# The sums of the down projection's weight quarters, made on GpSimd in place of VectorE

## What is computed

```
def conv_ffn(a, w_up, conv_w, w_down):
    g, u = jnp.split(dwconv3(a @ w_up, conv_w), 2, axis=-1)
    return (jax.nn.silu(g) * u) @ w_down
...
h = h + g2 * conv_ffn(modulate(rms_norm(h, norm_ffn[i]), sh2, sc2), ffn_w_up[i], ffn_conv[i], ffn_w_down[i])
```

## Time and profile before

| | before |
|---|---|
| median of three runs | 1985.34 us |
| the profiled execution | 1986.11 us, its span 1984.3 us |
| TensorE (PE) | 1875.4 us, 95% of the span |
| VectorE (DVE) | 909.3 us, 46% |
| ScalarE (ACT) | 371.8 us, 19% |
| GpSimd (POOL) | 25.1 us, 1% |
| DMA | 466.33 MB, 235 GB/s on the mean |
| granted clock of TensorE | 0.974 |

### The profile page before, as it was taken

The page is one execution under the profiler, slowest core; times in us unless marked ns, Lnnn a source line. Parts: engine busy times, 40 slices in busy tenths (PEclk is TensorE's granted clock), DMA queues, the critical chain, the costliest instruction groups (busy, mean ns, idle before and its releaser), DMA issues.

```text
span 1984.3 us, 45659 instructions
## 1 busy us (share of the span) xinstructions
PE 1875.4 (95%) x20976; PEld 1639.5 (83%) x20976; DVE 909.3 (46%) x1566; ACT 371.8 (19%) x691; POOL 25.1 (1%) x24
## 2 busy tenths in 40 slices
PE   6999987989998999997999998999999989999998
PEld 4788776889997688785989997667888988878898
DVE  3868786100004758765100004575667661134355
ACT  3012232100002022232100003163211101021110
POOL 0000200000000000200000000000000000000000
PEclk8999998999999999998999999999999999999999
DMA  9994547699995673543799994211878553435330
GB/s 359 387 386 157 192 167 282 234 361 404 423 413 202 220 261 129 204 178 133 300 388 410 423 405 149 85 43 43 283 270 296 199 206 119 136 127 170 122 113 23
DMA packets 180613, 466.33 MB, mean 235 GB/s; under 512 B 5152, under 2 KB 55680, under 8 KB 172288
## 3 DMA queue, kind: packets, MB, share of 16 engines
q1 hardware_dynamic: 180192, 463.83, 62.9%
q10 hardware_dynamic: 288, 0.52, 0.1%
HBM read 463.29 MB, written 1.05 MB: 234 GB/s over the span
## 4 chain that ended last, share of the span: by engine, by line
PE 87%; DVE 8%; ACT 2%; issue 1%; DMA 1%; SPq 0%; DVEq 0%; ACTq 0%
PE pair L395 86%; DVE AR L1557 1%; DMA ring<-in_ada_w 1%; PE pair L1034 1%; DVE RST L1612 1%; DVE AR L1795 1%; DVE XH L2186 1%; ACT AR L1279 1%; DVE XH L1557 1%; DVE AR L1805 0%; SPq L286 0%; PE pair L903 0%; DVE AR L1809 0%; DVE XH L1796 0%; DVE AR L1787 0%
## 5 line engine op out<-in xcount | busy, mean ns | idle before, releaser
L395 PE MATMUL pair<-XH,ring 128*128 128x256 f32 (+1 forms) x3328 | 751.4, 387 | 19.2 <-ACT XH L1180 17.3
L395 PEld LDWEIGHTS pair<-XH,ring 128*128 128x128 f32 (+1 forms) x3328 | 629.6, 191 | 126.0 <-issue 30.4
L395 PE MATMUL pair<-AR,ring 128*64 128x88 f32 (+2 forms) x14336 | 700.5, 249 | 19.0 <-issue 14.9
L395 PEld LDWEIGHTS pair<-AR,ring 128*64 128x64 f32 (+1 forms) x14336 | 670.8, 140 | 42.6 <-issue 22.9
L2044 DVE TENSOR_TENSOR AR<-AR,pair 128x352 f32<-128x352 f32 x32 | 16.7, 521 | 428.9 <-PE pair L395 428.9
L1557 DVE SCALAR_TENSOR_TENSOR AR<-ring,CACT,AR 128x512 f32<-128x512 f32 x245 | 184.2, 752 | 8.7
L395 PE MATMUL pair<-AR 128*64 128x128 f32 (+5 forms) x1472 | 145.4, 302 | 6.2 <-ACT AR L1446 3.3
L395 PEld LDWEIGHTS pair<-AR 128*64 128x64 f32 (+3 forms) x1472 | 116.2, 152 | 17.9 <-issue 4.2
L2242 DVE SCALAR_TENSOR_TENSOR AR<-pair,VEC,AR 128x255 f32<-128x255 f32 x88 | 41.9, 476 | 96.2 <-ACT AR L1471 96.2
L1379 ACT ACTIVATE AR<-pair 128x704 f32 (+1 forms) x32 | 24.4, 762 | 306.1 <-PE pair L395 306.1
L1471 ACT ACTIVATE AR<-pair,VEC 128x256 f32<-128x256 f32 x88 | 36.6, 467 | 217.9 <-PE pair L395 217.9
(11 more groups left out here) (268 smaller groups left out, 1199.9 us busy)
## 6 DMA issues: line engine op xcount, KB each, us to landing
ring<-in_ada_w SPq DMA_DIRECT2D x48, 2048.0 KB, 13.1
ring<-in_w_gate SPq DMA_DIRECT2D x32, 2048.0 KB, 10.4
ring<-in_w_up SPq DMA_DIRECT2D x32, 2048.0 KB, 10.6
ring<-in_w_down SPq DMA_DIRECT2D x32, 2048.0 KB, 11.3
ring<-in_ffn_w_up SPq DMA_DIRECT2D x44, 1024.0 KB, 7.6
ring<-in_w_in SPq DMA_DIRECT2D x18, 2048.0 KB, 14.4
ring<-in_ffn_w_down SPq DMA_DIRECT2D x8, 2048.0 KB, 8.0
ring<-in_sc_w_in SPq DMA_DIRECT2D x6, 2048.0 KB, 7.9
```

Source lines behind the costliest of these rows:

```text
L395: return pe.matmul(o, lhsT, rhs, start=start, stop=stop, **kw)
```

## The change

The function `weight_sums` and its calls are gone from VectorE's list. GpSimd's list gets, after its work in the first block, a wait for the last chunk of the attention's output weights, and then the same four sums for all twelve chunks, in one row and with the same buffers and semaphores.

```diff
-            def weight_sums(l, n, since=0, upto=4):
...
-                    if j == 20:
-                        weight_sums(l, 0)
...
                 token_sums(l, 2)
-                for n_ in (1, 2):
-                    weight_sums(l, n_)
-                weight_sums(l, 3, upto=3)
                 output(X, l, 0)
-                weight_sums(l, 3, since=3)
                 if l == 0:
                     for t in range(1, 4):
                         fold(H, t, t == 6)
-                for n_ in (4, 5):
-                    weight_sums(l, n_)
                 output(X, l, 1, H if l == 0 else None)
...
+            pool.wait_ge(s["multiplied"], ck("wwo", 1) + 1)
+            for l in range(DEPTH):
+                for n in range(6):
+
+                    i, c = 6 * l + n, ck(f"down{n}", l)
+                    n_p = DOWN_PAIRS[n % 3][1]
+                    a11, a12, a21, a22 = weight_blocks(c, n_p)
+                    s1, s2, s4 = [x[:, 0:n_p, :] for x in SX]
+                    pool.wait_ge(full[c % RING], 16 * (c // RING + 1 + extra(c)))
+                    if i:
+                        pool.wait_ge(s["sum_used"], i)
+                    pool.tensor_tensor(s1, a21, a22, ALU.add).then_inc(s["weights_summed"], 1)
+                    pool.wait_ge(s["weights_summed"], 4 * i + 1)
+                    pool.tensor_tensor(s2, s1, a11, ALU.subtract).then_inc(s["weights_summed"], 1)
+                    pool.tensor_tensor(a21, a11, a21, ALU.subtract).then_inc(s["weights_summed"], 1)
+                    pool.wait_ge(s["weights_summed"], 4 * i + 2)
+                    if i:
+                        pool.wait_ge(s["multiplied"], (c if n else ck("down5", 0) + 1))
+                    pool.tensor_tensor(s4, a12, s2, ALU.subtract).then_inc(s["weights_summed"], 1)
```

## The result

The changed kernel takes 1988.53 us, the median of 15 runs (1980.24 to 1994.67); the kernel before, in as many runs, 1980.23 us (1977.06 to 1986.54). The ratio is 1.0037, its 95% interval 1.0024 to 1.0050 (the two medians alone would give 1.0042): slower by 5 to 10 us. Forecast were 7.1 us and 0.36%. The profiled execution took 1993.53 us, its span is 1991.8 us, 7.5 us longer than that of before. In this profile lines from 2141 on are numbered otherwise: the sums are L2293 (s1), L2295 (s2), L2296 (a21) and L2300 (s4), `output` is L2166, and what was L2248 is L2226.

What follows compares the result with a forecast made beforehand. TensorE alone was taken to bound both down stages. Delays of 5.7 us, 0.8 ahead of the one-column matmuls and 0.6 of collisions made 7.1 us: 1992.4 us, 0.36% more; own range 1989 to 1995, with rivals 1984 to 2007.

Steps and rivals of the forecast that it cites:

- VectorE's freed time is worth nothing: Down stages: taking some 54 us of sums off VectorE gains no time by itself, as `output` waits for TensorE.
- 1.7 to 3 us over: Down stages: what VectorE's three sums, 4 us, left of the gap from product 2's start to the next product 6.
- T: Time of one two-input sum on GpSimd: 2.35 us for 1024 elements, 1.76 us for the short chunks' 768.
- Delays of 0.51, 1.81 and 0.51 us: TensorE late at product 6 of chunks 1, 3, 4 in each layer, from a 7.49 us chain; 5.7 us for both.
- the collision that was forecast at 0.3: Chunk 1: GpSimd's s1 and VectorE's L2139 wait for each other, 0.3 us in each layer, 0.6 in all.
- 0.8 us ahead of the one-column matmuls: First layer, near 1545 us: chunk 0's sums hold up VectorE by 3.5 to 3.9 us, TensorE by 0.8, once.
- `output` does not collide: Down stages: `output` reads PSUM and one SBUF input; collision taken as 0, with 1.2 us kept for the range.
- No cost for the clock: TensorE's new stalls of 0.5 to 1.8 us were counted as costing nothing in granted clock.
- A dearer sum: Rival: GpSimd's sum costs 2.51 us or more, making the kernel slower by over 0.5%; typically 1999 us; chance 0.33.
- the upper end: Dearest case for GpSimd's sum: 3.65 us (2.74 short), delays of 18.7 us a layer, 37 in all, 2024 us.
- The cheap sum: Rival: GpSimd's sum takes near 1.75 us, nothing is late; 1985.3 us, or 1986.7 with collisions; chance 0.15.
- the gain from VectorE: Rival: VectorE's freed 54 us gain at most 0.5 us at `output` after chunk 2; 1984.8 us; chance 0.06.

Runs made afterwards that it cites:

- e6: Changed kernel with two sets of sum buffers used in turn and chunk 0's sums waiting until the last modulation rows are summed; 1983.78 us, one run.
- e7: Kernel before, with s1 made twice on VectorE in each chunk; 1984.27 us, one run (kernel before beside it 1984.66).
- e1: Changed kernel with GpSimd's sums of chunk 0 waiting until VectorE has summed the last modulation rows; 1989.66 us, one run.
- e3: Changed kernel with s1 made twice on GpSimd in each chunk; 2029.58 us, ratio 1.0242 to the kernel before.
- e5: Kernel before, with only the in-place difference of a21 moved to GpSimd, s1, s2 and s4 on VectorE; 1983.71 us, one run (kernel before beside it 1984.66).

## Why the prediction was right, point by point

- *TensorE alone is the bound, VectorE's freed time is worth nothing.* Right. VectorE fell from 909.3 to 863.4 us busy (not by the whole 54 us, since its rows count standing still: over the whole execution 2.0 us more in L2226, 2.1 in L1555 and 2.2 in L2139), and `output` after chunk 2 is still released by TensorE, after 24.59 us of idle time. e6 has VectorE as free as the change does and no stretch shorter than before. One statement beside it was too wide: "1.7 to 3 us over" left out that VectorE has other work ahead of chunk 4's sums; e7 found about 1.5 us there. And one reading of the earlier trace rows was wrong: 1623.50 is not the end of chunk 5's last product but of product 5, and products 3 and 4 start at 1624.62 and 1625.93; `output` after chunk 5 begins beside them. Nothing in the sum hangs on it.
- *T = 2.35 us, 1.76 for short.* 2.36 and 1.81. That it came out so close was luck: two errors in the reasoning cancel. After the change the same COPY of 2048 elements took 1.89 us once, so its own cost is 0.92 ns an element at most and the 2.45 us of the earlier trace rows held waiting, as the text had suspected; and two inputs cost 2.30 ns an element, 2.5 times one, where the reasoning had twice. With 1.89 us in its formula T would have been 1.89, and only chunk 3 late, by 0.4 us. The Trainium skill's 4497 ns for 2048 elements (GPSIMD Engine Reference, section 3.1) gave an estimated 2.25 us, 0.11 below what the trace shows.
- *Delays of 0.51, 1.81 and 0.51 us, chunks 2 and 5 hidden.* Measured 0.81 (with the collision that was forecast at 0.3 and is 0.2), 1.91 and 0.60 in the first layer, nothing in 2 and 5. The chain is 7.59 us where 7.49 was computed: s1 comes 0.34 us after product 2's start in place of 0.29, TensorE 0.15 after the sum in place of 0.05, and the three sums with what lies between them take 7.10 in place of 7.15. Both down stages: 5.7 + 0.6 = 6.3 us forecast, 3.47 + 3.37 = 6.84 measured.
- *0.8 us ahead of the one-column matmuls.* Right place and cause (e1), 0.49 us. The collisions went otherwise than laid out: the two L2226 got in after GpSimd's second and third sums, and the one long stop, 2.57 us, was L1555's. VectorE lost 3.3 us in all (1.06 + 0.14 + 2.09), where 3.5 to 3.9 were laid out. L1555 reads one tensor and one value a partition from SBUF (L2220, which has such a value too but takes its tensor from PSUM and SBUF, kept its 0.47 us beside the sums); the exclusion of "two inputs" as the text had it is not the whole of it. The Trainium skill (SBUF — State Buffer, Who interferes with whom) has an exception that the prediction left out: a tensor-scalar operation in a two-port mode takes the same lock. The trace agrees as far as 2.57 against 0.48 us goes; the mode itself no row shows.
- *`output` does not collide.* Right: 6.33 us before and after, with three sums of 2.36 to 2.38 us beside it.
- *No cost for the clock.* Right for waits of up to 1.7 us: after the wait of 1.72 us the granted clock is 1.00 (1599.1 to 1602 us of the changed kernel). e3 shows that longer waits can cost it: see below.
- *Rivals.* A dearer sum was decided against by T; e3 confirms the formula behind it, but the 37 us computed for the upper end would probably have been more by a lower clock, which the formula leaves out. The cheap sum and the gain from VectorE did not occur.
- *The sum:* 7.1 us forecast, 7.4 in the stretches, 8.3 between the medians, 5 to 10 by the ratio's interval. The absolute 1992.4 us is 3.9 above the 1988.53 measured, just below its own range's 1989, since the three runs of the kernel before from which it starts had a median 5.1 us above that of fifteen (1985.34 against 1980.23). That is scatter of the starting point and no part of the mechanism.

## What to carry to other kernels

Before work is moved to a slower engine, measure the gap between the event that frees its buffer and the event that needs its result; the engine's throughput says little: here 9.4 us of sums in 14 us of products were late with one set of buffers and hidden with two. Look also at what the moved work meets in its new place in time: here GpSimd and VectorE stopped each other for up to 2.2 us an instruction. And time freed on an engine gains nothing where that engine was never waited for.

## What the runs showed of the hardware

- A two-input float32 sum on GpSimd is 2.36 us for 1024 elements a partition and 1.81 for 768 (2.15 ns an element and 0.16 us fixed), VectorE's 1.22 for 1024.
- A GpSimd row's duration includes its waiting for VectorE (3.40 us in e5 for a sum of 2.36), and so does a VectorE row its waiting for GpSimd (2.77 us for an L2139 of 0.56).
- Between two GpSimd sums in a row VectorE got in with one instruction each time that it waited (L2226 twice, L2139).
- In e3 a wait of 4.14 us was followed by products at clock 0.50 and cost 2.9 us more, one of 2.32 us (after matmuls at full pace) by a longer stretch of 3.4 us, and one of 3.04 us in the first layer by none, while its fellow of 2.98 in the second was followed by a slow product. So the wait's length alone does not tell; no run here shows what does.
